# Time mix's norm by token tile, with the keys of one tile projected before those of the next

## The reference

```python
def rms_norm(x, g):
    y = xf * lax.rsqrt(jnp.mean(xf * xf, axis=-1, keepdims=True) + RMS_EPS)
    return (y * g.astype(jnp.float32)).astype(x.dtype)

def rwkv7_time_mix(h, mu, w_in, ...):          # h = rms_norm(x, norm_a)
    xx = jnp.pad(h, ((0, 0), (1, 0), (0, 0)))[:, :-1] - h
    for i, wd in enumerate(widths):             # r, w, k, v, a, g
        outs.append((h + xx * mu[i]) @ w_in[:, off:off + wd])
        off += wd
```

## Time and profile before

| | us |
|---|---|
| median of 3 runs | 1495.8 |
| lowest, highest | 1493.16, 1495.95 |
| the profiled execution | 1495.62 |
| its span (first to last instruction) | 1493.8 |

### The profile page before, as it was taken

One profiled execution on the slowest core, in us unless ns is written; L12 is line 12 of the kernel. 1 busy time (PEld: TensorE's weight loads), 2 busy tenths in 40 slices (PEclk: granted clock), 3 DMA queues, 4 the chain that ended last, 5 costly groups with the idle time before them and its releaser, 6 DMA issues.

```text
span 1493.8 us, 19127 instructions
## 1 busy us (share of the span) xinstructions
PE 1330.1 (89%) x7300; PEld 878.0 (59%) x7300; DVE 828.7 (55%) x1996; ACT 420.1 (28%) x965; POOL 293.0 (20%) x269
## 2 busy tenths in 40 slices
PE   5999999999999999999999889998877777877775
PEld 2444799998588887888889645543333333333322
DVE  6406667455642344422214486678777877777654
ACT  1203322222052216355102333233222322222212
POOL 0000000000000010000001344556444443444420
PEclk9999999999999999999999999999999999999999
DMA  8344100054321624522344999999999999999994
GB/s 310 104 154 137 48 3 3 2 170 136 117 99 43 197 67 159 169 99 85 113 155 146 420 420 420 421 421 420 422 421 421 421 422 420 421 421 422 421 421 184
DMA packets 65111, 368.02 MB, mean 246 GB/s; under 512 B 7229, under 2 KB 8637, under 8 KB 31933
## 3 DMA queue, kind: packets, MB, share of 16 engines
q0 software_dynamic: 37152, 269.50, 43.5%
q1 hardware_dynamic: 27870, 97.31, 19.2%
HBM read 365.73 MB, written 1.05 MB: 246 GB/s over the span
## 4 chain that ended last, share of the span: by engine, by line
PE 62%; DMA 26%; DVE 8%; ACT 2%; issue 1%; POOL 0%; DVEq 0%; SPq 0%; POOLq 0%; ACTq 0%
DMA arena<-peer_in,arena 18%; PE bank L1603 15%; PE bank L2246 9%; PE bank L433 8%; DMA res<-peer_in,arena 7%; PE bank L1149 3%; PE bank L2196 3%; PE bank L535 3%; PE bank L1229 2%; PE bank L1206 2%; PE bank L1297 2%; PE bank L661 2%; DVE arena L2468 1%; PE bank L2184 1%; PE bank L1687 1%
## 5 line engine op out<-in xcount | busy, mean ns | idle before, releaser
L2246 PE MATMUL bank<-arena 128*128 128x512 f32 x580 | 272.5, 611 | 65.4 <-ACT arena L2337 65.3
L1603 PE MATMUL bank<-arena,ring 128*128 128x256 f32 (+2 forms) x1104 | 232.5, 371 | 5.5 <-DVE cst L2018 2.8
L2246 PEld LDWEIGHTS bank<-arena 128*128 128x128 f32 x580 | 108.0, 193 | 219.5 <-issue 219.2
L1603 PEld LDWEIGHTS bank<-arena,ring 128*128 128x128 f32 x1104 | 198.8, 190 | 34.5 <-DVE cst L2018 3.6
L2468 DVE CUSTOM_DVE_ANT_0 arena<-arena 128x1024 f32<-128x1024 f32 x145 | 175.8, 1222 | 53.6 <-DMA arena<-peer_in,arena 53.4
L2505 POOL DMA_INDIRECT arena<-peer_in,arena x145 | 164.1, 1132 | 177.9 <-PE bank L2246 161.3
L2337 ACT ACTIVATE arena<-cst,arena 128x128 f32<-128x128 f32 x256 | 88.8, 394 | 132.0 <-DVE arena L2418 128.6
L433 PE MATMUL bank<-ring,arena 128*128 128x512 f32 x256 | 114.1, 608 | 8.8 <-DVE arena L848 8.8
L2329 ACT ACTIVATE arena<-arena 128x2 f32<-128x2 f32 x128 | 37.8, 295 | 274.2 <-DVE arena L2468 274.0
L2246 PE MATMUL bank<-ring,arena 128*128 128x512 f32 x176 | 87.3, 639 | 25.8 <-ACT arena L2337 25.7
L433 PEld LDWEIGHTS bank<-ring,arena 128*128 128x128 f32 x256 | 49.9, 196 | 72.0 <-issue 72.0
(11 more groups left out here) (386 smaller groups left out, 1922.3 us busy)
## 6 DMA issues: line engine op xcount, KB each, us to landing
ring<-stream_in SPq DMA_DIRECT2D x160, 512.0 KB, 3.4
ring<-stream_in SPq DMA_DIRECT2D x8, 384.0 KB, 6.1
arena<-peer_in,arena POOLq DMA_INDIRECT x145, 34.2
row<-rows_in SPq DMA_DIRECT2D x4, 512.0 KB, 18.9
cst<-cst_in SPq DMA_DIRECT2D x1, 1933.0 KB, 18.8
res<-res_in SPq DMA_DIRECT2D x2, 544.0 KB, 4.3
row<-rows_in POOLq DMA_DIRECT2D x2, 512.0 KB, 6.1
cst<-rg_w_in SPq DMA_DIRECT2D x1, 1024.0 KB, 7.6
```

The costliest lines, as they stand in the source:

```text
L1603: mm = nc.tensor.matmul(bank[:, first:first + width], slot[:, at + k * cols:at + (k + 1) * cols], src[:, k, :], start=k == 0, stop=k == kt ...
L2246: mm = nc.tensor.matmul(core.banks[2 * t + b][:, :], diag[i % ND], value_half(i, b), start=first, stop=last)
```

## The change

The work of the first stage is cut by token tile instead of by half of the feature tiles.

- **Loads.** SP loads token tile 0 of all 8 feature tiles first (144 columns: the 16 extra and 128 tokens, 8 runs of 576 bytes a partition), then `vec`, the ones, and token tile 1 (8 runs of 512 bytes a partition).
- **ACT.** It begins with a Sqrt on one column, so that the table of Sqrt is loaded at the start; in the built program no further table load stands between it and the Squares. Then two Squares of 512 columns for each token tile, and a Sqrt of 128 columns for each token tile, the first of them queued behind all four Squares.
- **PE.** The sum for tile 0 is still one matmul behind the tree, now with 128 columns; for tile 1 there is no tree: eight matmuls of 128 columns add up in the bank. Both stand ahead of the keys. Then both halves of the keys for tile 0, and both for tile 1; the weight slots are given back in the pass of tile 1. The number of key matmuls stays 32 (64 passes), all of 128 x 512.
- **DVE.** `gain` multiplies x by the norm's weights before the root is known (one instruction of 1024 elements a partition for each tile, output to `hn`); `gain(1)` stands behind the tree and ahead of the reciprocal of tile 0. `norm_and_mix(t)` takes the reciprocal over 128 tokens and then, two feature tiles at a time, scales `hn`, forms `xx` and the mixture of keys. The other mixtures are as before.
- One bank more is claimed, so the rotation is one bank further on for the rest of the program.

```diff
@@ PE @@
-        bank = claim(pe, "ss_a")
+        bank = claim(pe, ("ss_a", 0))
         pe.wait_ge(tree_sum.handle, 1)
-        nc.tensor.matmul(bank[:, 0:T], cst("ones"), squares[:, 0, :], start=True, stop=True).then_inc(*full("ss_a"))
+        nc.tensor.matmul(bank[:, 0:P], cst("ones"), squares[:, 0, 0:P], start=True, stop=True).then_inc(*full(("ss_a", 0)))
+        bank = claim(pe, ("ss_a", 1))
+        for k in range(KT):
+            pe.wait_ge(squared.handle, 3 + k // 4)
+            mm = nc.tensor.matmul(bank[:, 0:P], cst("ones"), squares[:, k, P:T], start=k == 0, stop=k == KT - 1)
+        mm.then_inc(*full(("ss_a", 1)))
+
+        def project_keys(t):
+            for half in range(2):
+                bank = claim(pe, ("k", t, half))
+                for kp in range(KT // 2):
+                    slot = core.weights(pe, ("k", half, kp))
+                    for i in range(2):
+                        k = 2 * kp + i
+                        if not half:
+                            pe.wait_ge(mixed.handle, t * KT + k + 1)
+                        mm = nc.tensor.matmul(bank[:, :], mix["k"][:, k, t * P:(t + 1) * P], slot[:, i * 512:(i + 1) * 512],
+                                              start=k == 0, stop=k == KT - 1)
...
-        project(0, "k")
+        for t in range(TT):
+            project_keys(t)
@@ ACT @@
-        for n in range(2):
-            at = slice(n * KT // 2, (n + 1) * KT // 2)
-            act.wait_ge(g.x_loaded[n].handle, 16)
-            nc.scalar.activation(squares[:, at, :], x[:, at, :], ACT.Square).then_inc(*squared.up())
         act.wait_ge(g.eps_set.handle, 1)
-        bank = filled(act, "ss_a")
-        nc.scalar.activation(rstd, bank[:, 0:T], ACT.Sqrt, bias=g.eps[:, 0:1], scale=1.0 / D).then_inc(*free("ss_a"))
+        nc.scalar.activation(g.eps[:, 2:3], g.eps[:, 0:1], ACT.Sqrt)
+        for t in range(TT):
+            act.wait_ge(g.x_loaded[t].handle, 16)
+            for n in range(2):
+                at, cols_t = slice(n * KT // 2, (n + 1) * KT // 2), slice(t * P, (t + 1) * P)
+                nc.scalar.activation(squares[:, at, cols_t], x[:, at, cols_t], ACT.Square).then_inc(*squared.up())
+        for t in range(TT):
+            bank = filled(act, ("ss_a", t))
+            nc.scalar.activation(rstd[:, t * P:(t + 1) * P], bank[:, 0:P], ACT.Sqrt, bias=g.eps[:, 0:1], scale=1.0 / D)\
+              .then_inc(*free(("ss_a", t)))
@@ DVE @@
+        def gain(t):
+            at = VEC_AT["norm_a"][0]
+            by_feature = g.vec[:, at:at + KT].unsqueeze(2).to_broadcast([P, KT, P])
+            dve.wait_ge(g.x_loaded[t].handle, 16)
+            lk(nc.vector.tensor_tensor(hn[:, :, t * P:(t + 1) * P], x[:, :, t * P:(t + 1) * P], by_feature, ALU.mult))
...
@@ SP @@
-        for n in range(2):
-            at = slice(n * KT * S // 2, (n + 1) * KT * S // 2)
-            sp.dma_start(g.res[:, at], g.res_in[:, at]).then_inc(*g.x_loaded[n].dma())
         first = 2 * P
+        tiles_in = [(tiles(g.res, S)[:, :, at], tiles(g.res_in, S)[:, :, at]) for at in (slice(0, NM + P), slice(NM + P, S))]
+        sp.dma_start(*tiles_in[0]).then_inc(*g.x_loaded[0].dma())
+        sp.dma_start(g.vec, g.vec_in).then_inc(*g.vec_loaded.dma())
         sp.dma_start(g.cst[:, 0:first], g.cst_in[:, 0:first]).then_inc(*g.ones_loaded.dma())
-        sp.dma_start(g.vec, g.vec_in).then_inc(*g.vec_loaded.dma())
+        sp.dma_start(*tiles_in[1]).then_inc(*g.x_loaded[1].dma())
```

More of the change, by code:

```diff
@@ L698, in take @@
                       .then_inc(*free((name, t, half)))
-        take("k", K)
+        for t in range(TT):
+            for half in range(2):
+                bank = filled(act, ("k", t, half))
+                nc.scalar.activation(tok(K, t)[:, half * 512:(half + 1) * 512], bank[:, :], ACT.Copy).then_inc(*free(("k", t, half)))
         bank = filled(act, ("lora", "w"))
@@ L828, in _ @@
+        first = squares[:, :, 0:P]
+        dve.wait_ge(g.vec_loaded.handle, 16)
+        gain(0)
         dve.wait_ge(squared.handle, 1)
-        nc.vector.tensor_tensor(squares[:, 0:2, :], squares[:, 0:2, :], squares[:, 2:4, :], ALU.add)
+        nc.vector.tensor_tensor(first[:, 0:2, :], first[:, 0:2, :], first[:, 2:4, :], ALU.add)
         dve.wait_ge(squared.handle, 2)
-        lk(nc.vector.tensor_tensor(squares[:, 4:6, :], squares[:, 4:6, :], squares[:, 6:8, :], ALU.add))
-        lk(nc.vector.tensor_tensor(squares[:, 0:2, :], squares[:, 0:2, :], squares[:, 4:6, :], ALU.add))
@@ L833, in _ @@
[L833 to L838, removed]
-                                                 op0=ALU.mult, op1=ALU.mult)
-        lk(ins)
-        nc.vector.tensor_scalar(xx[:, :, 0:1], hn[:, :, 0:1], -1.0, None, ALU.mult)
@@ L842, in _ @@
-        for n in range(4):
-            at = slice(2 * n, 2 * n + 2)
-            ins = nc.vector.tensor_tensor(xx[:, at, 1:T], hn[:, at, 0:T - 1], hn[:, at, 1:T], ALU.subtract)
-            if n == 0:
-                lk(ins)
-                for j in range(2):
-                    nc.vector.scalar_tensor_tensor(out=mix["k"][:, j, :], in0=xx[:, j, :], scalar=vec("mu", 2 * KT + j),
-                                                   in1=hn[:, j, :], op0=ALU.mult, op1=ALU.add).then_inc(*mixed.up())
@@ L850, in _ @@
-        lk(ins)
-        for name, n in (("k", 2), ("w", 1), ("a", 4), ("v", 3), ("r", 0), ("g", 5)):
+        lk(nc.vector.tensor_tensor(first[:, 4:6, :], first[:, 4:6, :], first[:, 6:8, :], ALU.add))
+        lk(nc.vector.tensor_tensor(first[:, 0:2, :], first[:, 0:2, :], first[:, 4:6, :], ALU.add))
+        nc.vector.tensor_tensor(first[:, 0, :], first[:, 0, :], first[:, 1, :], ALU.add).then_inc(*tree_sum.up())
+        gain(1)
+        norm_and_mix(0)
+        norm_and_mix(1)
+        for name, n in (("w", 1), ("a", 4), ("v", 3), ("r", 0), ("g", 5)):
@@ L1078, in _ @@
         pool.wait_ge(g.eps_set.handle, 1)
-        filled(pool, "ss_a")
+        for t in range(TT):
+            filled(pool, ("ss_a", t))
         nc.gpsimd.memset(unit[13][LORA:LORA + 1, 0:2 * T], 1.0).then_inc(*ones_set.up())
```

34 lines of the change are left out of this document (27 added, 7 removed).

## The result

The changed kernel takes 1486.6 us (median of 4 runs, 1484.3 to 1487.6) against 1495.5 of the kernel before (4 runs, 1493.2 to 1496.0), a ratio of 0.9945 with a 95% interval of 0.9933 to 0.9958: 8.9 us less, with 1487.4 forecast. Two later lots on other occasions gave 1483.5 against 1492.8 (0.9940, interval 0.9927 to 0.9954) and 1486.7 against 1492.9 (0.9952, interval 0.9940 to 0.9965). The profiled execution took 1487.56, its span 1485.7 instead of 1493.8.

What follows compares the result with a forecast made beforehand. PE was taken as the bound, 89% busy, so the last key's end counts: 48.8 to 40.6 us, 8.2 less. Profiled 1495.6 - 8.2 gives 1487.4 us, range 1485.0 to 1491.2.

Steps and rivals of the forecast that it cites:

- Arrival of x: Loads at the start: tile 0 lands at 5.3 us, vec at 5.5, tile 1 at 7.6.
- The term of 5.5 ns a packet: Loads of x: extra cost of short rows on each DMA engine, 0.35 us for each tile.
- the first of the two bounds: Short-row price in the loads of x: 5.5 ns a packet from bytes moved, chosen over 84 ns from vec's landing.
- rival 2: x lands later: 47 ns a packet, time 1489 to 1491, chance 0.15; 84 ns, sum about zero, 0.04.
- First mixture and first key: Start: first mixture done at 12.05 us; tile 1's 16 sum passes end at 12.7, when keys start.
- The keys: 64 key passes: PE never waits for DVE; 27.45 us if the slow phase is spent, ending at 40.6 with 0.5 added.
- a rise somewhat inside the keys: Key passes: allowance of 0.5 us for PE reaching its fast level only after the keys start.
- Rival 1: Slow phase runs again in the keys: they end at 42.3, saving 6.4 us, time 1489.2; chance 0.15.
- 2 and 3: Later x, and slower than before: the latter has 100 ns a packet, x at 17.2, time 1497.8; chance 0.04.
- Behind the keys: After the keys: DVE's wait for PE at the LoRA shrinks from 19.6 to about 10 us, still covering its work.
- rival 4: Gain at 40 us given back behind 117 us by slow phases, or at the banks: about 1494; chance 0.05.
- At the banks: Moved bank rotation, at the transposes behind block attention: 0 to 0.2 us lost.

Runs made afterwards that it cites:

- keys by slot: Changed kernel with each weight slot again used for both token tiles before the next, norm still by tile: 1494.3 us, ratio 1.0002 to the kernel before.
- the table alone: Kernel before plus only a one-column Sqrt at ACT's start, loading its table before x lands: 1493.8 against 1494.3 us, ratio 0.9993.
- table and early work in the kernel before: Kernel before plus early Sqrt table and four matmuls on zeros right behind its sum of squares: 1490.7 against 1492.9 us, ratio 0.9979.
- early work: Changed kernel with tile 1's sum in bank 7, plus four matmuls on zeros while PE waits for x: median 1484.8 against 1486.6 us over both lots.

## Why the prediction held, step by step

**Arrival of x.** Tile 0 at 5.05 (5.3 said), tile 1 at 8.12 (7.6 said). The windows of after (last columns: clock, DMA share, GB/s), to be held against the earlier trace rows:

```profile
3.00:4.00 1.00, 0.00 (x0) 0.00 (x0) 0.00 (x0) 0.00 (x0) 0.00 (x0) 1.00 1.11 353
5.00:6.50 1.50, 0.00 (x0) 0.00 (x0) 1.18 (x1) 1.15 (x2) 0.00 (x0) 1.00 0.97 290
```

Rows of 576 bytes went at about 350 GB/s, and the stretch with the vector parameters, the ones and tile 1's rows of 512 bytes at 290 (326 and 331 in the kernel's other two profiles), with the DMA engines taken up wholly, where long rows reach 418. The term of 5.5 ns a packet was somewhat too large for tile 0 (an estimate from the windows: at 350 GB/s a packet takes 26.3 ns on its engine, 4.3 more than at 418). For tile 1 it was right in size: in eight profiles with these loads, of four kernels beside the changed one, tile 1 was there between 7.24 and 8.32, and 7.6 lies among them; the first profile is one of the two late ones. Choosing the first of the two bounds was right, the 47 ns of rival 2 lay far off. The Trainium skill (DMA: Bandwidth & Descriptors, the table at its start) gives 512 bytes as the least for line rate; this trace disagrees, with 290 and 350 against 418 (and 331 at most for the later stretch in the other profiles). The error of 0.5 at tile 1 cost nothing: its squares are needed by the sum at 8.84, and the first were ready in time; the Sqrt of tile 0, queued behind them, ran at 9.18 against 9.25 forecast.

**First mixture and first key.** Reciprocal 9.63 to 10.58, first mixture written at about 12.1 (12.05 said). The 16 passes of the sum end at 12.59 and bind, by 0.4 us; said was 12.7, by 0.5. The kernel with the sum behind the first key shows that they are well placed there: 0.4 us of start against 1.1 of slow key passes.

**The keys.** DVE delivers a pair each 1.44 (1.47 said), PE has no hole in 64 passes. Two sizes of this step were off. 64 passes at the fast level are 27.70, not 27.45: a quarter of a microsecond more than 64 times the spacing, once for the lot. And the slow passes left in the keys cost 0.71 (0.40 and 0.25 in the other profiles) where I added 0.5. Here are after's weight loads, to be held against the earlier trace rows:

```profile
13.29 0.34 PEld L434 LDWEIGHTS bank<-ring,arena 128*128 128x128 f32 x1 [0.52 <-issue]
14.14 0.27 PEld L434 LDWEIGHTS bank<-ring,arena 128*128 128x128 f32 x1 [0.52 <-issue]
14.66 0.19 PEld L434 LDWEIGHTS bank<-ring,arena 128*128 128x128 f32 x1 [0.24 <-issue]
```

The slow passes end about 6 us after PE's first work (8.28), between the weight load at 14.14, which is half slow, and the one at 14.66. The prediction counted on the 4.15 us of the kernel before and added 0.5 for a rise somewhat inside the keys. In the other two profiles of the same kernel the slow stretch was 5.5 and 4.9 us (to 13.76 and 13.30), so its length is not a constant of the kernel. What saves the keys is that the first four microseconds of it are the sum's. With -0.1 at the start, +0.25 and +0.2 the end is 41.0 instead of 40.6. Rival 1 (42.3) did not come, nor did 2 and 3, for which tile 1 would have had to land after 9.

**Behind the keys.** DVE's wait for the LoRA projection is 11.6 us (about 10 said), so its cover holds:

```profile
44.63 3.26 DVE L901 SCALAR_TENSOR_TENSOR arena<-arena,vec 128x256 f32<-128x256 f32 x8 [11.63 <-PE bank L471]
```

Nothing was given back that stays (rival 4). At the banks I named 0 to 0.2; 0.06 belongs to them, and 0.24 more to the clock in one profile. From the expert layer's first query to the end the span has 693.4 before and 693.8, 692.8 and 692.9 after. The span is 8.1 us shorter where the keys end 7.8 sooner: 0.3 is lost at the transposes and 0.6 won in the stretch behind L1342 (24.12 instead of 24.70), which takes between 23.3 and 24.95 in the thirteen profiles.

**Sum.** 1487.56 in the profiled execution against 1487.4 forecast. That it agrees to a tenth is luck: the keys' end was 0.4 off in this profile and right in the other two (40.5), the stretch behind L1342 happened to give 0.6 back, and profiles scatter by 1.7 us at the g projection alone. The gain of the medians was 8.9, 9.3 and 6.2 us on the three occasions, where 8.2 was forecast.

## What to carry to other kernels

When an engine waits at the start for a long elementwise chain, cut the chain by tiles of the dimension that the matmuls can also be ordered by, and order the matmuls so that all work on the first tile comes ahead of the second; the cut with the old order gave nothing here that the times could tell, and with the new order 8 us. Price a start not by its first pass but by its last: TensorE begins slow, and its slow passes came back behind a hole of 4.7 us, so matmuls that have to be done anyway are best put into the hole, even where they hold the start back a little (here 0.4 us against 1.1). And hold a forecast of a few microseconds against the scatter of the stages it does not touch before trusting its total.

## What the runs showed of the hardware

- TensorE's slow passes at the start (twice the spacing, 1.2 instead of 2.4 GHz) lasted from at most 3.95 to over 6.6 us from the start of its work, read by the first weight load of 0.19 us: at most 3.95 in the kernel with keys by slot (8.28 to 12.23), 4.2 in the long run of keys of before and 5.1 with the table alone (both from the first key pass), 5.2 with table and early work in the kernel before, 6.4, 5.5 and 4.9 in the three profiles of the changed kernel, and over 6.6 in the second profile with early work, where eight passes of 128x512 without a hole, from 1.47 to 8.10, were all slow. The same kernel differs by 1.5 us from run to run.
- Behind idle times of 1.45 us (early work) and 2.04 (early work in the kernel before) passes that had been fast stayed fast; behind 4.71 (keys by slot) they were slow again. With the sum behind the first key, PE had not yet been fast when it went idle for 3.18 us, so that row does not tell how long a hole may be. The Trainium skill (TensorE: Matmul & The Clock Gate, Part 1) says that idle is the throttled state and that the point of release varies from run to run; both agree with these rows.
- The granted clock in the windows does not show the slow passes at the very start: it reads 1.00 in this window of the kernel with early work, in which every pass is slow. Later it does show them: 0.50 behind the hole of 4.71 us, and 0.57 and 0.50 in the g projection of two profiles. So the prediction was right to go by the spacing at the start, but could have read the clock at the g projection.

```profile
2.00:7.00 5.00, 5.00 (x7) 1.94 (x6) 1.71 (x3) 1.38 (x4) 0.00 (x0) 1.00 1.00 299
```

- A stretch in which TensorE never stops can lose its clock too: behind 32 matmuls with a single moving column (128x1, L499) the clock fell to 0.50 in eleven of thirteen profiles. That the small matmuls are the cause was not tried.
- Early work on zeros makes TensorE's later passes fast as real work does, and it delayed nothing visible: in its first profile DVE began with tile 0 at 5.25 (5.32, 5.30 and 5.42 without it), in its second at 5.38.
- Rows of 576 bytes went at 342 to 353 GB/s. Why the stretch with rows of 512 bytes went slower still (290, 326 and 331 GB/s in three profiles, with two smaller loads among them) was not tried and stays open.
